# A two-block kernel: both Fourier transforms split once by parity, with the sums and differences on GpSimd

## The reference, cut to what matters

```python
def _fourier_mix(u, w_f):
    B, S, _ = u.shape                       # S = 256
    ug = u.reshape(B, S, N_FOURIER_GROUPS, FOURIER_GROUP_DIM).astype(jnp.float32)   # 4 groups of 256
    re = jnp.fft.fft2(ug, axes=(1, 3), norm="ortho").real.astype(u.dtype)
    y = jnp.einsum('bsgc,gce->bsge', re, w_f)
    return y.reshape(B, S, FOURIER_WIDTH)
```

## Time and profile before

| | |
|---|---|
| median of 3 runs | 2312.27 us (2309.9 to 2316.16) |
| profiled execution, own time | 2315.37 us |
| its span | 2313.7 us |
| TensorE busy | 2285.5 us |
| VectorE busy | 1541.7 us |
| ScalarE busy | 1107.6 us |
| GpSimd busy | 146.2 us |
| mean granted clock of TensorE | 0.996 |
| Fourier and attention stage | 196.3 to 240.7 us of the span |

### The profile page before, as it was taken

The page is one execution under the profiler, slowest core; times in us unless marked ns, Lnnn a source line. Parts: engine busy times, 40 slices in busy tenths (PEclk is TensorE's granted clock), DMA queues, the critical chain, the costliest instruction groups (busy, mean ns, idle before and its releaser), DMA issues.

```text
span 2313.7 us, 29249 instructions
## 1 busy us (share of the span) xinstructions
PE 2285.5 (99%) x10475; PEld 1881.4 (81%) x10475; DVE 1541.7 (67%) x1835; ACT 1107.6 (48%) x1517; POOL 146.2 (6%) x213
## 2 busy tenths in 40 slices
PE   8999999999999999999999999999999999999998
PEld 7888888888888888878878877787888888888886
DVE  6987658877877877886767664556545544555556
ACT  5445445545545545545563463545443344434444
POOL 1110001111111111110011000000000000000000
PEclk9999999999999999999999999999999999999999
DMA  9884458888888888886677663564555665556553
GB/s 322 297 283 167 128 182 306 310 293 279 277 298 266 270 301 270 272 274 214 214 248 239 212 214 124 183 225 149 197 182 191 208 198 186 192 190 199 184 182 127
DMA packets 245899, 523.77 MB, mean 226 GB/s; under 512 B 20096, under 2 KB 20496, under 8 KB 244496
## 3 DMA queue, kind: packets, MB, share of 16 engines
q1 hardware_dynamic: 214256, 405.32, 53.5%
q0 software_dynamic: 29568, 111.97, 13.9%
q10 hardware_dynamic: 1952, 4.85, 0.6%
HBM read 517.87 MB, written 4.21 MB: 226 GB/s over the span
## 4 chain that ended last, share of the span: by engine, by line
PE 95%; DVE 2%; ACT 1%; issue 1%; DMA 0%; DVEq 0%; ACTq 0%; POOLq 0%
PE acc L1661 29%; PE acc L1663 29%; PE acc L1662 29%; PE tp L1703 2%; DVE wlo L992 1%; PE m L1714 1%; DVE macc L1022 1%; PE tp L2020 0%; PE tp L2038 0%; PE tp L2032 0%; PE tp L1945 0%; PE acc L1687 0%; PE acc L1685 0%; PE acc L1686 0%; DMA mring<-w_mod 0%
## 5 line engine op out<-in xcount | busy, mean ns | idle before, releaser
L992 DVE TENSOR_TENSOR wlo<-wring,whi 128x1024 fp32r<-128x1024 f32 x764 | 918.8, 1213 | 588.2 <-ACT whi L501 474.8
L501 ACT ACTIVATE whi<-wring 128x1024 fp32r<-128x1024 f32 (+1 forms) x510 | 532.1, 1047 | 732.2 <-PE acc L1663 731.0
L1661 PE MATMUL acc<-whi,xhi 128*128 128x512 f32 x2096 | 827.3, 395 | 8.0 <-DVE wlo L992 3.1
L1663 PE MATMUL acc<-whi,xlo 128*128 128x512 f32 x2096 | 818.2, 390 | 0.0
L1662 PE MATMUL acc<-wlo,xhi 128*128 128x512 f32 x2096 | 817.4, 390 | 0.0
L1661 PEld LDWEIGHTS acc<-whi,xhi 128*128 128x128 f32 x2096 | 394.7, 188 | 99.3 <-issue 13.8
L1663 PEld LDWEIGHTS acc<-whi,xlo 128*128 128x128 f32 x2096 | 394.3, 188 | 83.4
L1662 PEld LDWEIGHTS acc<-wlo,xhi 128*128 128x128 f32 x2096 | 394.9, 188 | 80.1 <-issue 0.7
L511 ACT ACTIVATE whi<-wring 128x1024 fp32r<-128x1024 f32 x266 | 281.0, 1059 | 319.5 <-PE acc L1663 319.3
L1022 DVE SCALAR_TENSOR_TENSOR macc<-mring,csil,macc 128x512 f32<-128x512 f32 x480 | 344.0, 746 | 31.4 <-DMA mring<-w_mod 25.2
L1661 PE MATMUL acc<-whi,ahi 128*128 128x512 f32 x608 | 238.9, 393 | 1.2 <-DVE wlo L992 1.2
(11 more groups left out here) (254 smaller groups left out, 1191.8 us busy)
## 6 DMA issues: line engine op xcount, KB each, us to landing
wring<-w_up SPq DMA_DIRECT2D x216, 512.0 KB, 4.6
wring<-w_down SPq DMA_DIRECT2D x216, 512.0 KB, 5.0
mring<-w_mod POOLq DMA_DIRECT2D x192, 512.0 KB, 5.1
wring<-w_in SPq DMA_DIRECT2D x184, 512.0 KB, 5.4
wring<-w_gate SPq DMA_DIRECT2D x88, 512.0 KB, 4.4
wring<-w_out SPq DMA_DIRECT2D x64, 512.0 KB, 4.8
gbig<-ctx_in POOLq DMA_DIRECT2D x2, 1024.0 KB, 8.4
hspill<-h ACTq DMA_DIRECT2D x1, 2048.0 KB, 8.0
```

What stands on the lines that cost most here:

```text
L501: act.activation(whi[:, piece_slot(c, piece), 0:half], wring[:, g4, piece * half:(piece + 1) * half], ACT.Copy).then_inc(hi_done, 1)
L992: dve.tensor_tensor(wlo[:, h4, 0:half], wring[:, g4, piece * half:(piece + 1) * half], whi[:, h4, 0:half].bitcast(F32), ALU.subtract).then ...
L1661: pe.matmul(dst, hi[:, tile, rows], whi[:, h4, w], start=(kg == first and k == 0), stop=False)
L1663: last = pe.matmul(dst, lo[:, tile, rows], whi[:, h4, w], start=False, stop=(kg == final and k == KG - 1))
```

## The change

The transform over positions (F1) is split by parity of the frequency: for an even frequency the table's two halves of positions are equal, for an odd one they are opposite. So GpSimd forms the sum and the difference of proj's two tiles of positions once for all groups (the sum in place, the difference in pdiff), and TensorE multiplies the sum with the table of even frequencies and the difference with that of odd ones, each with 128 columns and one tile: 4 matmuls for a group where there were 8. The results are written to every second column of acc, so that the frequencies stand in the order of before. The compact tables tab_s are copied by GpSimd from tab_f.

The transform over channels (F2) is split in the same way: GpSimd forms fsplit, sum and difference of fpos's two halves, for each group, and TensorE multiplies with one tile of weights read at every second column of tab_f: again 4 matmuls for 8. The even channels come out in one half and the odd ones in the other, and w_fourier is loaded in that order. The split of proj stands in GpSimd's program between the third and the fourth block of mod loads, those of fpos behind the fourth.

```diff
--- before.py
+++ after.py
@@ -153,6 +153,9 @@
             tab_a = sb("tab_a", [P, 2, T * S], scope=ph)
             proj = sb("proj", [P, T, 8 * NB], scope=ph)
             wf = sb("wf", [P, FGROUPS, 2, FDIM], scope=ph)
+            pdiff = sb("pdiff", [P, FGROUPS * FDIM], scope=ph)
+            tab_s = sb("tab_s", [P, 2, S // 2], scope=ph)
+            fsplit = sb("fsplit", [P, 2, S], scope=ph)
             qkT = sb("qkT", [P, 2, 2, S], scope=ph)
             nmax = sb("nmax", [P, HEADS, T], scope=ph)
             aden = sb("aden", [P, HEADS, T], scope=ph)
@@ -257,6 +260,9 @@
         h_added = sem("h_added")
         h_scaled = sem("h_scaled")
         proj_set = sem("proj_set")
+        proj_split = sem("proj_split")
+        tab_split = sem("tab_split")
+        f_split = sem("f_split")
         f1_done, f1_copied, f2_done, f2_kept, f2_mirrored, f3_done, f3_hi, f3_lo = (
             sem(n) for n in ("f1_done", "f1_copied", "f2_done", "f2_kept", "f2_mirrored", "f3_done", "f3_hi", "f3_lo"))
         qk_turned, qk_copied, scores_done, scores_biased, max_set, exps_done = (
@@ -430,7 +436,7 @@
             pool.dma_start(tab_f[:, :, :], fourier_tables).then_inc(misc_in, 16)
             pool.dma_start(tab_a[:, :, :], attn_tables).then_inc(misc_in, 16)
             for g in range(FGROUPS):
-                pool.dma_start(wf[:, g, :, :], w_fourier[g].rearrange("(c p) e -> p c e", p=P)).then_inc(misc_in, 16)
+                pool.dma_start(wf[:, g, :, :], w_fourier[g].rearrange("(p c) e -> p c e", c=2)).then_inc(misc_in, 16)
             w_mod_v = w_mod.rearrange("(s k p) n -> s p k n", k=2, p=P)
 
             def mod_block(kind, i, per_step, last_step):
@@ -443,8 +449,30 @@
                     c.add("m")
                     c.add("ma", per_step)
 
-            with c.loop(pool, 4, m=8, ma=32) as i:
+            with c.loop(pool, 3, m=8, ma=32) as i:
                 mod_block(SH1, i, 4, 4)
+
+            pool.wait_ge(misc_in, 16 * 6)
+            pool.tensor_copy(tab_s[:, 0, 0:FCOS // 2 + 1], tab_f[:, 0, 0:FCOS:2]).then_inc(tab_split, 1)
+            pool.tensor_copy(tab_s[:, 0, FCOS // 2 + 1:S // 2], tab_f[:, 0, S + 2:S + S // 2:2]).then_inc(tab_split, 1)
+            for two in range(2):
+                pool.tensor_copy(tab_s[:, 1, two * S // 4:(two + 1) * S // 4],
+                                 tab_f[:, 0, two * S + 1:two * S + S // 2:2]).then_inc(tab_split, 1)
+
+            mixed = slice(0, FGROUPS * FDIM)
+            pool.wait_ge(proj_set, 2 + 2)
+            pool.tensor_tensor(pdiff[:, :], proj[:, 0, mixed], proj[:, 1, mixed], ALU.subtract).then_inc(proj_split, 1)
+            pool.wait_ge(proj_split, 1)
+            pool.tensor_tensor(proj[:, 0, mixed], proj[:, 0, mixed], proj[:, 1, mixed], ALU.add).then_inc(proj_split, 1)
+            mod_block(SH1, 3, 4, 4)
+
+            for g in range(FGROUPS):
+
+                pool.wait_ge(f1_copied, g + 1)
+                if g:
+                    pool.wait_ge(f2_done, g)
+                for half, op in ((0, ALU.add), (1, ALU.subtract)):
+                    pool.tensor_tensor(fsplit[:, half, :], fpos[:, 0, :], fpos[:, 1, :], op).then_inc(f_split, 1)
 
             mod_block(SC2, 0, 2, 4)
             pool.wait_ge(tp_free, 2 + 16)
@@ -682,7 +710,7 @@
                 if s < HEADS and s % 2 == 0:
                     act.wait_ge(f1_done, g + 1)
                     if g:
-                        act.wait_ge(f2_done, g)
+                        act.wait_ge(f_split, 2 * g)
                     act.activation(fpos, acc[:, 0, :].rearrange("p (c s) -> p c s", c=2), ACT.Copy).then_inc(f1_copied, 1)
                 if s % 2:
                     act.wait_ge(f2_done, g + 1)
@@ -1772,6 +1800,8 @@
 
             pe.wait_ge(proj_set, 2 + 7)
             pe.wait_ge(misc_in, 16 * 6)
+            pe.wait_ge(tab_split, 4)
+            pe.wait_ge(proj_split, 2)
             for s in range(HEADS + 1):
                 g = s // 2
                 if s < HEADS:
@@ -1788,22 +1818,20 @@
                         pe.wait_ge(f1_copied, g)
                     for ct in range(2):
                         cols = slice(g * FDIM + ct * P, g * FDIM + (ct + 1) * P)
-                        for at, table, n in ((0, 0, FCOS), (FCOS, S + 1, S - FCOS)):
-                            for t in range(T):
-                                last = pe.matmul(acc[:, 0, ct * S + at:ct * S + at + n], proj[:, t, cols],
-                                                 tab_f[:, t, table:table + n], start=(t == 0), stop=(t == T - 1))
+                        freqs = acc[:, 0, ct * S:(ct + 1) * S].rearrange("p (f two) -> p two f", two=2)
+                        pe.matmul(freqs[:, 0, :], proj[:, 0, cols], tab_s[:, 0, :], start=True, stop=True)
+                        last = pe.matmul(freqs[:, 1, :], pdiff[:, cols], tab_s[:, 1, :], start=True, stop=True)
                     last.then_inc(f1_done, 1)
                 if s % 2:
 
-                    pe.wait_ge(f1_copied, g + 1)
+                    pe.wait_ge(f_split, 2 * (g + 1))
                     if g:
                         pe.wait_ge(f2_mirrored, g)
                     for cc in range(2):
                         for part, at, n in ((0, 0, FCOS), (1, FCOS, S - FCOS)):
-                            for ct in range(2):
-                                last = pe.matmul(m0[:, cc * S + at:cc * S + at + n],
-                                                 tab_f[:, ct, part * 2 * S + cc * P:part * 2 * S + (cc + 1) * P],
-                                                 fpos[:, ct, at:at + n], start=(ct == 0), stop=(ct == 1))
+                            last = pe.matmul(m0[:, cc * S + at:cc * S + at + n],
+                                             tab_f[:, 0, part * 2 * S + cc:part * 2 * S + S:2],
+                                             fsplit[:, cc, at:at + n], start=True, stop=True)
                     last.then_inc(f2_done, 1)
                 if s == HEADS:
                     pe.wait_ge(f3_lo, FGROUPS - 2)
```

## The result

The kernel after took 2317.26 us (median of 19 runs) against 2312.46 us for the kernel before (19 runs taken beside them): ratio **1.0019, interval 1.0012 to 1.0025**, that is 4.4 us slower, between 2.8 and 5.8. The forecast was 2311.3, 1.0 us faster than before, in a range from 2307.5 to 2318.0. The time lies in the range, but it moved the other way than was forecast; the move is short of the 0.3% that the chances were told by. One of the 19 executions after took 9211 us: it is left out of the ratio, and the median without it is 2317.2.

What follows compares the result with a forecast made beforehand. TensorE was taken to bound the kernel, with the stage's even steps bound by TensorE and odd ones by the softmax. Terms -1.6 + 0.6 + 0 = -1.0 us from the median 2312.27 gave 2311.3 us, range 2307.5 to 2318.0.

Steps and rivals of the forecast that it cites:

- what GpSimd adds ahead of the stage: Before the Fourier and attention stage: GpSimd's copies and 1024-column operations delay a load issue by 2.5 us, costing 0 us.
- the first group, to X(2): Stage start: group 0's split is late behind the eighth load issue, TensorE idles 4 us; +0.6 us, F1(1)'s saving inside.
- F1 in the even steps s=4 and 6: Even steps, bound by TensorE: halved F1 lets the scores come earlier, 0.8 us per step taken, -1.6 us.
- F2 in the odd steps: Odd steps, bound by the softmax: halved F2 only lengthens TensorE's wait for the scaling, 0.27 to some 1.2 us; saves nothing.
- the exclusion rival: Ahead of the stage: VectorE stands while GpSimd reads SBUF; 3.3 us reach TensorE, giving 2314.6 us; chance 0.28.
- the clock rival: Odd steps: TensorE's clock falls in waits grown to 1.2 us, 1.6 us per fall; three falls give 2316.1 us; chance 0.12.
- Prices of GpSimd: GpSimd's added operations: 0.7 us for 256 columns, 2.5 us for 1024, copies 0.1 to 0.25 us each.
- Strides: F1's PSUM writes and F2's weight reads at every second element: taken as 0; rival, PSUM's stride eats F1's saving, 2313.6, chance 0.05.

Runs made afterwards that it cites:

- e7: Kernel after the change, with VectorE taking the head's remainder ahead of the mirroring in odd steps; 2316.33 us, ratio 1.0012 to the kernel before.
- e1: Kernel after the change with F2 put back as before, so F1's half alone; 2313.07 us against 2314.05, ratio 0.9998 to the kernel before.
- e3: Kernel after the change, with group 0's split on GpSimd ahead of the last modulation load; 2315.71 us, ratio 1.0014 to the kernel before.
- e5: Kernel before, with three unused 1024-column subtractions on GpSimd behind the third block's load issues; single run 2317.39 us against 2314.05.
- e6: Kernel before, with nine 1024-column memsets of a spare tile on GpSimd behind the third block's load issues; single run 2314.10 us against 2314.05.
- e8: Kernel after the change with projection split later, group 0's split ahead of the last modulation load, and remainder first; 2314.14 us, ratio 0.9999 to before.
- e9: Kernel after the change with F2 as before, the projection split later and the remainder first; 2311.53 us against 2313.80, ratio 0.9994 to the kernel before.
- e10: Kernel before, with only VectorE's head remainder moved ahead of the mirroring, as a control; 2312.75 us, ratio 0.9998 to the kernel before.
- e2: Kernel after the change with F1 put back as before, so F2's half alone; 2315.15 us, ratio 1.0007 to the kernel before.
- e4: Kernel after the change, with the projection split between the second and third modulation load of the last block; 2315.37 us, ratio 1.0010 to before.

## Why the prediction was wrong

By its own steps, against the mean of each kernel's three profiled executions:

| step | forecast, us | measured, us |
|---|---|---|
| what GpSimd adds ahead of the stage | 0 | +1.8 |
| the first group, to X(2) | +0.6 | +2.0 |
| F1 in the even steps s=4 and 6 | -1.6 | -0.5 |
| F2 in the odd steps | 0 | 0 |
| not located in a stretch | | +1.1 |

- **The step that failed first: "What GpSimd adds ahead of the stage: 0 us".** It asked only whether GpSimd's own queue would be late, and that was near enough: the issue moved by 4.5 us (163.25 to 167.72; forecast 165.7, of which 0.6 has no row behind it) and cost nothing ahead of the stage, as the memsets show. But the operations keep VectorE from its own while they read. This was the exclusion rival, with a chance of 0.28, and right in kind: its reserve of 1.4 us was exact (3.2 late on VectorE, 1.8 on TensorE). Its price of 3.3 came out at 1.8, since part of the first operation fell into VectorE's idle time for the modulation load (1.65 us). The row to weigh had been: VectorE just behind a wait for a load, with four modulation operations and a remainder to do before TensorE can go on.
  The Trainium skill, SBUF — State Buffer, § Who interferes with whom, gives the exclusion as a rule, and the trace agrees: 2893 against 737 ns on VectorE, 5.68 against 2.77 us on GpSimd, and nothing beside memsets. The same section names tensor_scalar, with one tensor input, among the instructions that can take the shared ports in a two-port mode; here too it was held (5.17 us for two). The prediction took over only the part on two inputs.
- **The first group.** The mechanism was as forecast (the split behind the eighth issue, F2(0) near 205, TensorE idle for some 4 us), and two sizes were off. F2(0) began at 206.58, of which 1.9 is the delay from ahead of the stage (T(0), the stage's first transposes, at 198.22; the stage began at 196.30 before). And the low stretch did not lie as it did: forecast 205 to 209, about as long as the one in the earlier trace rows, it lasted to 212.1. Against the kernel before in an execution that has its fall, T(0) to X(2) is 0.9 longer (18.14 against 17.25), near the 0.6. But that fall is chance there: without it the kernel before takes 15.68 and 15.66, and the mean difference is 18.21 less 16.20. The forecast named that price ("Without the low stretch it would be -1") on the wrong side: what had to be without it was before, not after.
- **F1 in even steps.** It gave 0.24 us each, not 0.8. The forecast followed the scores S to their operands and found 0.84 in hand, and did not follow W, which stands ahead of S. W writes the part of PSUM that VectorE's remainder of the head before, L1222, reads, and VectorE does that behind the mirroring. W had some 0.5 us in hand in the kernel before. e7 shows that nothing else is short: with the remainder first the step is 5.49, 0.68 less than before and 0.1 from the forecast.
- **F2 in odd steps:** as forecast, 4.83 us from X to X. The grown wait lies in two places, 0.27 for the query and key copy and 0.59 for the scaling, not 1.2 in one. So the clock rival, which needed a stand over 1.07 us there, had no place: the clock is at 1.00 from 214 to 240. Its bracket of 1.07 to 1.79 us doesn't hold either: 1.79 left the clock at 1.00 in seven of ten executions (last section), and in the kernel before the stand of 1.07 is followed by stands of 1.49 and 2.04 us, within the last of which the clock fell (0.51 from 1571 to 1578).
- **Prices of GpSimd:** 256 columns 0.70 to 0.80 us each (forecast 0.7), 1024 columns 2.75 (2.5). The four copies took 0.69 to 1.00, not 0.1 to 0.25; they ran beside VectorE's operations of 0.74.
- **Strides:** F1's records, which write every second column of PSUM, are 0.11 us apart (222.12 to 222.34 for two), F2's, which read every second weight, too. The Trainium skill, SBUF — State Buffer, § Door 1, would have had the first slow; the trace doesn't show it.

All three errors had the same sign. With the exclusion in the sum at its measured 1.8, the forecast would have been 2313.1, 0.8 slower than before and so on the side on which it came out; with W's wait (+1.1) and the first group as measured (+1.4) as well, 2315.6, 3.3 slower. That the time lay within the range is no merit of the mechanism: the range reached that far up for the exclusion and part of the clock rival.

## What to carry to other kernels

Work on GpSimd that reads SBUF was here not done beside VectorE's two-input operations and its TENSOR_SCALAR but in turn with them (memsets were done beside them): before placing it, find in VectorE's timeline where TensorE's next need is furthest off, and put it there (the same two operations cost 1.8 us in one place and 0 a few us later). When a product on TensorE is shortened, follow the operands of everything that stands behind it, not only of the next long wait. And where a stage has a stand after which the clock sometimes falls, profile both kernels several times before reading a difference of 1 us off one pair.

## What the runs showed that was not expected

- **The hold goes both ways, and to one-input operations.** GpSimd's split of the projection took 5.68 us beside VectorE's remainders, and its copies of 64 columns up to 1.00 us; VectorE's TENSOR_SCALAR of 512 columns took 2.6 us instead of 0.44. That the copies were stretched by the same hold is read from the timelines and wasn't tried apart.
- **The same short stand is followed by a fall of the clock in some executions and not in others.** A stand of 1.79 us before X(1) stood in ten profiled executions (before three times, e1, e3, e5, e6, e8, e9, e10). In three of them (before once, e5, e6) the clock fell to 1.2 GHz at its end, which made C of the kernel before longer by 1.6 us; in seven it stayed at 2.4 GHz, although e3 and e8 had two more stands of over 1 us just ahead. The stands ahead of it differ between the kernels (S(1) stood 1.49 and 1.29 us in e5 and e6), but not within the kernel before, which shows both cases. With the stand of 3.78 to 3.94 us ahead of F2(0) the clock fell, within it or just behind, in all six executions that had it (after three times, e2, e4, e7). The low stretch lasted some 7 us in four of them and 3.5 in e4 and e7; what decides between the two was not found.
- **Strided operands of TensorE cost nothing** here: 128-column records at 0.11 us with an output of every second PSUM column, and the same with weights at every second element.
